# Pooling mixer: the product ahead of the trailing means, ScalarE copies gates and keys, half a u block between gates

## The chip, the cores and the metric

One core of one Trainium2 chip runs the whole program. The metric is the device time of one execution in microseconds (us); the number given for a kernel is the median of several runs. TensorE (PE) does matmuls and transposes, VectorE (DVE), ScalarE (ACT) and GpSimd (POOL) the elementwise work, SyncE (SP) starts most transfers. Each engine has its own instruction stream, and they wait for each other through semaphores (`wait_ge`, `then_inc`).

## The reference, cut to what matters

The program is one inference step of a two-layer encoder trunk on 544 tokens of 1,024 features: 512 frames of a new stream (prompt) and 32 frames of a running one (sample). Layer 0 mixes by a gated MLP (A) next to a sliding-window attention (B), layer 1 by trailing means (C). A SwiGLU FFN follows each mixer. Around each part stand an RMSNorm before and one after.

```python
def spatial_gate(u, va, ws, bs):                       # mixer A
    z = einsum('hij,bnjhc->bnihc', masked(ws), va) + bs
    return u * z
def pool_mixer(xn, hist, pos, c_w, c_scale):           # mixer C; hist: 15 older frames (zeros for the prompt)
    ext = concatenate([hist, xn])
    cs = pad(cumsum(ext))
    for g, w in enumerate((2, 4, 8, 16)):              # four groups of 256 features
        win_sum = cs[HIST+1 : HIST+1+t, g] - cs[HIST+1-w : HIST+1-w+t, g]
        diffs[g] = win_sum / minimum(pos + 1, w) - xn[:, g]
    return einsum('btgc,gce->btge', diffs, c_w) * c_scale, ext[-15:]
h = h + rms_norm(pool_mixer(rms_norm(h, g0)), g1)
h = h + rms_norm((silu(x @ w_gate) * (x @ w_up)) @ w_out, g3)      # x = rms_norm(h, g2)
```

The mean over a window is linear in the frames and the product with `c_w` is linear in the features, so either may come first.

## The kernel before, in words

**Products.** All data is f32. A matrix is split into a high and a low part, and `product` (lines 574 to 576) issues three matmuls: high by high, high by low, low by high. Features lie on the 128 partitions, tokens along the columns. The tokens are cut into half a (256 frames) and half b (256 frames and the 32 of the sample, 288 columns).

**Weights.** Weights come in units of 8 blocks of 128 columns. SP loads a unit into `raw` (3 buffers); ACT's `hi_part(m)` (L1124) rounds it into `whi`, DVE's `lo_part(m)` (L1541) forms `wlo` as the difference (4 buffers each). When PE is through with unit m, ACT and DVE prepare unit m + 4.

**Passes and slots.** After the front (mixers A and B of layer 0) come the FFN passes: `gu` (gate and up products) and `fo` (product with `w_out`), each over one half, for layer 0 `gu` a, `gu` b, `fo` a, `fo` b, for layer 1 `gu` a, `gu` b, `fo` b, `fo` a. One unit of a pass is a slot. What else has to be done in a pass is hung between its slots by the table `STAGE`: for a norm s (1: before mixer C, 2: before the FFN of layer 1) and a half, it names the slot of each step, and `stepper` lets each engine run the steps that are due after its part of a slot (`LATER` is half a slot later, on ACT). Steps of one engine thus stand in its stream behind the unit's own work, and a step that waits holds up what stands behind it.

- `sum`, `spread`, `fold`, `pre`, `again`: sums of squares by matmuls with ones, and the `spread` of 1/rms over the partitions by matmuls with the identity (L841).
- `scale` and `x`: DVE scales two feature tiles (L1837); ACT rounds them to `xhi`, DVE's `x_low` (L1846) forms `xlo`.
- `rows`, `keep`, `bands`: the pooling of mixer C. `turn_rows` (L973) transposes h on PE to frames on the partitions, ACT's `keep_rows` (L1439) scales it by 1/rms into `rows_a`, `rows_b`; PE's `band` (L996 to L1001; L989 for the sample with its history) multiplies with constant band matrices, which gives mean minus frame, back with features on the partitions. ACT's `band_high` and DVE's `band_low` split it. Half a does this in the `fo` pass of half b of layer 0 (norm 1, half a), half b in the `gu` pass of half a of layer 1.
- `pool_products`: two units of `c_w` (`c` units), placed in the pass by `C_AFTER`; a tile of its output goes through a ring of PSUM banks (`POOL_RING`, four for half a and three for half b) and is evacuated by ACT's `evacuate_z`, which also writes the squares for the next norm.

**Front.** PE does the blocks of va, then five heads q0 to q3 and k (`r` = 0 to 4), with transposes of v, `ws`, the key cache and the new keys between them. DVE applies the rotation of each head in `rope_step(r)`. `gate(a)` is PE's product of va with `wm_t`; DVE's `bias_gate(a)` adds the bias. Gates 0 and 1 stand after head 3, gates 2 and 3 after head 4 (gate 3 waits until `bias_gate(0)` has freed bank 0); then comes the loop over attention chunks, in which PE does scores, transposes and values of a chunk, and between them steps of the u block (`u_step`, six matmuls each, as many as `U_STEPS` says), and DVE `shift`, ACT the exponentials. `fill(n, bank)` (L592) issues n matmuls of the identity whose result nobody reads.

Lines of before that the steps below touch:

```python
fill(FILL_ROPE, 7)                 # PE, r == 3
pe.wait_ge(wm_ready, 1)
pe.wait_ge(kc_ready, 1)
...
dve.tensor_copy(wm_t[0:CHUNK, :, :], turned[0:CHUNK])          # DVE, rope_step(2)
dve.tensor_copy(wm_t[CHUNK:P, :, CHUNK:P], turned[CHUNK:P, :, CHUNK:P]).then_inc(wm_ready, 1)
dve.tensor_copy(k_s[:, CHUNK:P], flat(5, 0, CHUNK)).then_inc(kc_ready, 1)
...
bias_gate(2)
bias_gate(3)
lo_part(13)                        # then the loop with shift(c)
```

Of the kernel before, what the change touches and what calls it, by code (L numbers as in the profile page):

```python
# [60 lines left out]
U_STEPS = (3, 3, 2, 3, 3, 2, 3, 3, 2, 4, 4)  # L61
# [3 lines left out]
GATE_BANKS = (0, 2, 4, 0)  # L65
# [15 lines left out]
FILL_ROPE, FILL_GATE, FILL_TAIL = 20, 5, 4  # L81
# [4 lines left out]
BAND_ENTRIES = (tuple(range(KC)), (0, 1, 2, 3, "sample", 4, 5, 6, 7))  # L86
CARRY = 16
# [69 lines left out]
KEPT = {(0, 0): 1, (0, 1): 2, (1, 0): 3, (2, 0): 4, (2, 1): 5, (3, 0): 6}  # L157
# [49 lines left out]
def shape_constants():  # L207
# [11 lines left out]
    return np.concatenate([np.eye(P, dtype=np.float32), cos, sin, pooling_matrices()], axis=1)  # L219


def pooling_matrices():


    j, i = np.arange(P)[:, None], np.arange(P + CARRY)[None, :]
    row_at = np.concatenate([np.arange(DEC), np.arange(-HIST, 0)])[:, None]
    first, later, sample = [], [], []
    for w in POOLS:
        inside = (j <= i) & (j > i - w)
        count = np.where(i < P, np.minimum(i + 1, w), w)  # L230
        first.append(inside / count - (i == j))
        later.append(inside / w - (i == j))
        rows = np.zeros((P, DEC))
        at = np.arange(DEC)[None, :]
        rows[:DEC + HIST] = ((row_at <= at) & (row_at > at - w)) / w - (row_at == at)
        sample.append(rows)
    return np.concatenate(first + later + sample, axis=1).astype(np.float32)


def build(nc, x_prompt, x_sample, cache_k, cache_v, state, norm_g, ab_w_in, ln_g, ln_b, a_ws, a_bs, b_sinks,  # L240
          ab_w_out, c_w, c_scale, ffn_w_in, ffn_w_out, constants,
          y_p, y_s, bk_p, bv_p, cp_p, bk_s, bv_s, cp_s, av_s):
    with ExitStack() as ctx:
# [327 lines left out]
        def _(pe):  # L571
# [374 lines left out]
            def ring_wait(b, n):  # L946
# [3 lines left out]
                if back < 0:  # L950
                    return
# [1164 lines left out]
```

## Time and profile before

| | |
|---|---|
| median of three runs | 1049.93 us (1049.64, 1049.93, 1051.5) |
| profiled execution | 1051.53 us, of which the span of instructions is 1049.2 us |
| PE busy | 1031.9 us (98% of the span) |
| DVE busy | 621.2 us (59%) |
| ACT busy | 514.4 us (49%) |
| POOL busy | 48.1 us (5%) |
| mean granted clock of PE | 0.998 of full speed |
| moved by DMA | 162.47 MB, mean 155 GB/s |

Times in rows of the trace count from the start of the span. A row in order of time gives the start, the length from the first instruction's begin to the last one's end, the engine, the line of the kernel, the operation, `out<-in` by the program's names, the shapes, the number of instructions, and in brackets the idle time before it with what ended it. Matmuls overlap in the array, so a matmul's own length (0.28 us for 256 columns) is longer than its turn in the stream. Fills and gates count two instructions for each of their matmuls.

### The profile page before, as it was taken

Reading aid. Unit: us, or ns where it says so; the run is one execution under the profiler, and the core shown is the slowest. Engines: PE = TensorE matmul, PEld = TensorE weight load, DVE = VectorE, ACT = ScalarE, POOL = GpSimd, SP = SyncE. Lnnn points to the kernel's source line nnn. Section 1 sums busy time; section 2 is a strip of 40 time slices with the busy share of each in tenths; the row PEclk is TensorE's granted clock in tenths of the full one; section 3 lists DMA queues with packets and bytes.
Section 4 is the critical chain, followed back from the end, with each engine's and each line's share of the span. In section 5 each row is a group of like instructions: output and inputs, shape, how many; then the busy total and the mean of one; then the engine's idle time right before and its main releaser. Section 6 shows DMA issues by size and latency. Waiting matters only on the chain.

```text
span 1049.2 us, 19401 instructions
## 1 busy us (share of the span) xinstructions
PE 1031.9 (98%) x8097; PEld 1013.4 (97%) x8097; DVE 621.2 (59%) x923; ACT 514.4 (49%) x846; POOL 48.1 (5%) x52
## 2 busy tenths in 40 slices
PE   7999999999999999999999999999999999999997
PEld 6898799899999999999999999999999999999997
DVE  5397854887555555545465777557854555444643
ACT  6622365655444444444457565565544444444552
POOL 0080210000000000000000000200000000000000
PEclk9999999999999999999999999999999999999999
DMA  8322122566666555546664586445665555455554
GB/s 273 82 75 76 42 61 82 159 183 181 184 190 171 165 166 169 164 133 184 181 185 121 163 229 191 127 141 168 184 173 164 168 169 153 136 167 167 158 163 151
DMA packets 307925, 162.47 MB, mean 155 GB/s; under 512 B 14586, under 2 KB 304354, under 8 KB 307839
## 3 DMA queue, kind: packets, MB, share of 16 engines
q1 hardware_dynamic: 307374, 160.78, 52.7%
q8 instruction: 64, 1.05, 0.4%
q0 software_dynamic: 224, 0.35, 0.1%
q14 instruction: 23, 0.18, 0.1%
q10 hardware_dynamic: 240, 0.10, 0.0%
HBM read 158.63 MB, written 2.58 MB: 154 GB/s over the span
## 4 chain that ended last, share of the span: by engine, by line
PE 91%; DVE 5%; ACT 1%; issue 1%; DMA 1%; POOL 0%; ACTq 0%; DVEq 0%
PE ps L574 29%; PE ps L576 28%; PE ps L575 28%; DVE wlo L1541 1%; PE ps L830 1%; PE ps L841 1%; DMA gain_rows<-in_c_scale_dram 1%; PE ps L1001 0%; PE ps L973 0%; PE ps L996 0%; DVE va L1606 0%; DVE s_sb L1715 0%; DVE top L1709 0%; DVE den L1725 0%; DVE tmp L1837 0%
## 5 line engine op out<-in xcount | busy, mean ns | idle before, releaser
L1541 DVE TENSOR_TENSOR wlo<-raw,whi 128x1024 fp32r<-128x1024 f32 (+2 forms) x332 | 369.6, 1114 | 272.1 <-ACT whi L1124 271.7
L574 PE MATMUL ps<-xhi,whi 128*128 128x288 f32 (+1 forms) x1600 | 465.7, 291 | 3.0 <-DVE xlo L1846 1.6
L575 PE MATMUL ps<-xlo,whi 128*128 128x288 f32 (+1 forms) x1600 | 461.5, 288 | 0.0
L576 PE MATMUL ps<-xhi,wlo 128*128 128x288 f32 (+1 forms) x1600 | 459.1, 287 | 0.0
L1124 ACT ACTIVATE whi<-raw 128x1024 fp32r<-128x1024 f32 (+2 forms) x332 | 316.2, 955 | 229.0 <-PE ps L576 214.6
L574 PEld LDWEIGHTS ps<-xhi,whi 128*128 128x128 f32 x1600 | 301.2, 188 | 6.0 <-DVE xlo L1846 2.0
L576 PEld LDWEIGHTS ps<-xhi,wlo 128*128 128x128 f32 x1600 | 302.1, 189 | 0.0
L575 PEld LDWEIGHTS ps<-xlo,whi 128*128 128x128 f32 x1600 | 301.5, 188 | 0.0
L574 PE MATMUL ps<-mhi_b,whi 128*128 128x288 f32 x352 | 104.9, 298 | 0.0
L576 PE MATMUL ps<-mhi_b,wlo 128*128 128x288 f32 x352 | 104.3, 296 | 0.0
L575 PE MATMUL ps<-mlo_b,whi 128*128 128x288 f32 x352 | 102.7, 292 | 0.0
L574 PE MATMUL ps<-mhi_a,whi 128*128 128x256 f32 x352 | 99.9, 284 | 0.0
L576 PE MATMUL ps<-mhi_a,wlo 128*128 128x256 f32 x352 | 99.5, 283 | 0.0
L575 PE MATMUL ps<-mlo_a,whi 128*128 128x256 f32 x352 | 99.2, 282 | 0.0
L1386 ACT ACTIVATE tmp<-ps 128x256 f32<-128x256 f32 (+1 forms) x88 | 34.9, 397 | 124.4 <-PE ps L576 120.1
L575 PEld LDWEIGHTS ps<-mlo_b,whi 128*128 128x128 f32 x352 | 67.0, 190 | 0.0
L574 PEld LDWEIGHTS ps<-mhi_a,whi 128*128 128x128 f32 x352 | 66.6, 189 | 0.0
L575 PEld LDWEIGHTS ps<-mlo_a,whi 128*128 128x128 f32 x352 | 66.4, 189 | 0.0
L574 PEld LDWEIGHTS ps<-mhi_b,whi 128*128 128x128 f32 x352 | 66.2, 188 | 0.0
L576 PEld LDWEIGHTS ps<-mhi_b,wlo 128*128 128x128 f32 x352 | 66.0, 187 | 0.0
L576 PEld LDWEIGHTS ps<-mhi_a,wlo 128*128 128x128 f32 x352 | 66.0, 187 | 0.0
L1914 DVE TENSOR_TENSOR tmp<-tmp,ps 128x256 f32<-128x256 f32 (+1 forms) x88 | 38.5, 437 | 37.4 <-PE ps L576 37.3
(219 smaller groups left out, 932.6 us busy)
## 6 DMA issues: line engine op xcount, KB each, us to landing
raw<-in_ffn_w_in_dram SPq DMA_DIRECT2D x176, 512.0 KB, 3.9
raw<-in_ffn_w_out_dram SPq DMA_DIRECT2D x64, 384.0 KB, 3.5
raw<-in_ffn_w_out_dram SPq DMA_DIRECT2D x64, 320.0 KB, 3.1
raw<-in_ab_w_in_dram SPq DMA_DIRECT2D x10, 512.0 KB, 4.4
raw<-in_ab_w_out_dram SPq DMA_DIRECT2D x10, 256.0 KB, 2.9
raw<-in_ab_w_out_dram SPq DMA_DIRECT2D x20, 128.0 KB, 3.1
x_tok<-in_x_prompt_dram SPq DMA_DIRECT2D x4, 512.0 KB, 7.3
raw<-in_ab_w_in_dram SPq DMA_DIRECT2D x8, 256.0 KB, 3.8
```

The lines of the kernel that those rows point to most:

```text
L574: pe.matmul(out, wh, xh, start=first, stop=False)
L575: pe.matmul(out, wh, xl, start=False, stop=False)
L576: return pe.matmul(out, wl, xh, start=False, stop=last)
L830: mm = pe.matmul(flat(6 + b, i, 1, n), acc[:, 0, t0:t0 + n], ones[:, :], start=True, stop=True)
L841: mm = pe.matmul(flat(6 + b, P + i * P, w), lhs, ident[:, P - w:P], start=True, stop=True)
L1124: act.activation(whi[:, m % NSPLIT, 0:n], raw[:, m % NRAW, 0:n], ACT.Copy).then_inc(w_hi, 1)
L1386: act.activation(tmp[:, f % 2, c], flat(bank, 0, n), ACT.Silu).then_inc(silu_done, 1)
L1541: dve.tensor_tensor(wlo[:, s, 0:n], raw[:, m % NRAW, 0:n], whi[:, s, 0:n].bitcast(F32), ALU.subtract)\
L1914: dve.tensor_tensor(tmp2[:, f % 2, c], tmp[:, f % 2, c], flat(bank, 0, n), ALU.mult)\
```

## The change

**Mixer C.** The product with `c_w` now comes first, on the normalised frames, and the trailing means are formed from its output with the features on the partitions. Norm 1 gets steps like those before an FFN (`again`, `x`: DVE scales by the gains and 1/rms, ACT and DVE split), and the `c` units follow. ACT copies each output tile into `wide_a` or `wide_b`, behind 15 columns of history (POOL: zeros for half a, the last 15 columns of half a for half b). DVE's `window_step` adds a shifted copy 1, 2, 4, 8 columns back: one step for the first group, four for the last. `mix` scales the sum and subtracts the product itself (for half a after a multiplication of the first 15 columns with tabled counts), ACT's `mixed_out` writes the scaled result and its squares, `add_z` the sums. All of `rows`, `keep`, `bands` and their PE transposes and band matmuls go, with their constants. For the sample, its 15 frames of history are loaded as rows, turned by `turn_hist` and appended to half b's operand, which gets 304 columns; `turn_rows` remains for the 64 last frames alone, which are an output, and POOL scales them. The `c` units stand earlier in their passes (`C_AFTER`), and the steps of norms 1 and 2 lie in other slots.

**Front.** ACT copies `wm_t` and `k_s` after its `hi_part(10)`; DVE no longer does. The two fills of 20 and 5 go. Four steps of the u block (half of one block of features) are put between gate 2 and gate 3, which writes bank 6 and waits for no bias; the loop has four u steps fewer in all.

```diff
-U_STEPS = (3, 3, 2, 3, 3, 2, 3, 3, 2, 4, 4)
+U_FIRST = 4
+U_STEPS = (2, 2, 2, 3, 2, 2, 2, 3, 2, 4, 4)
...
-GATE_BANKS = (0, 2, 4, 0)
+GATE_BANKS = (0, 2, 4, 6)
...
-C_AFTER = ((15, 16), (22, 24))
+X_GAIN = ((0, 2), (1, 0), (1, 2))
+LAST_ROWS = 2 * DEC
+Z_COLS = (HIST + P * 2, 2 * HIST + P * 2 + DEC)
+C_AFTER = ((11, 12), (18, 20))
 STAGE = {
-    (1, 0): {"sum": 0, "spread": 1, "scale": (1, 2, 3, 4), "fold": 6, "pre": 8, "rows": (7, 7, 8, 8),
-             "keep": (9, 9, 10, 10), "bands": (11, 11, 12, 12, 13, 13, 14, 14)},
-    (2, 0): {"sum": 20, "spread": 21, "scale": (21, 22, 23, 24), "fold": 26, "pre": 28, "again": 29,
-             "x": (29, 30, 31, 32)},
-    (1, 1): {"sum": 2, "spread": 4, "scale": (4, 5, 7, 8), "fold": 10, "pre": 12, "rows": (10, 11, 11, 15, 15, 16),
-             "keep": (14, 14, 15, 15, 16, 16), "bands": (17, 17, 18, 18, 19, 19, 20, 20, 21)},
-    (2, 1): {"sum": 28, "spread": 30, "scale": (30, 31, 33, 34), "fold": 36, "pre": 38, "again": 40,
-             "x": (40, 41, 42, 43)},
+    (1, 0): {"sum": 0, "spread": 1, "scale": (1, 2, 3, 4), "fold": 5, "pre": 7, "again": 8, "x": (8, 9, 10, 11),
+             "windows": (13, 15, 16), "ends": (14, 17), "post": (14, 15, 17, 18), "add": (15, 17, 18, 20)},
+    (2, 0): {"sum": 22, "spread": 23, "scale": (23, 24, 25, 26), "fold": 28, "pre": 29, "again": 30,
+             "x": (30, 31, 32, 33)},
+    (1, 1): {"sum": 2, "spread": 4, "scale": (4, 5, 7, 8), "fold": 10, "pre": 12, "again": 14, "x": (14, 15, 16, 17),
+             "hist": 9, "rows": (10, 11), "keep": (15, 16),
+             "windows": (20, 23, 24), "ends": (21, 25), "post": (21, 22, 25, 26), "add": (22, 24, 26, 27)},
+    (2, 1): {"sum": 29, "spread": 31, "scale": (31, 32, 34, 35), "fold": 37, "pre": 39, "again": 41,
+             "x": (41, 42, 43, 44)},
...
+                if UNITS[m] == ("gu", 1, 0, 4):
                     sp.wait_ge(w_used, FO_PASS[0, 1][-1] + 1)
...
+                    sp.dma_start(hist[0:HIST, :], state[0, 0]).then_inc(hist_loaded, 16)
+                    sp.dma_start(hist[HIST:HIST + 1, :], state[0, 0, HIST - 1:HIST, :]).then_inc(hist_loaded, 16)
+                    sp.dma_start(gain_row[:, :], norm_g[1, 0].partition_broadcast(LAST_ROWS)).then_inc(hist_loaded, 16)
...
-                if a < 3:
-                    pe.wait_ge(rope_cosined, a + 2)
-                else:
-                    pe.wait_ge(gate_biased, 1)
+                pe.wait_ge(rope_cosined, a + 2)
...
-                    fill(FILL_ROPE, 7)
-                    pe.wait_ge(wm_ready, 1)
+                    pe.wait_ge(wm_ready, 2)
...
-                    fill(FILL_GATE, bank)
...
-                        pe.wait_ge(gate_biased, 4)
+                        pe.wait_ge(gate_biased, 1)
...
+            for n in range(U_FIRST):
+                u_step(n)
+            gate(3)
...
+            def turn_hist():
+                pe.wait_ge(hist_loaded, 48)
+                for k in range(KC):
+                    mm = pe.transpose(flat(4, k * DEC, HIST + 1), hist[:, k * P:(k + 1) * P], ident[0:HIST + 1, 0:HIST + 1])
+                mm.then_inc(hist_turned, 1)
+            def turn_rows(i):
+                pe.wait_ge(h_added[1], 8)
+                if i:
+                    pe.wait_ge(hist_lo, 1)
                 for q in range(4):
+                    mm = pe.transpose(flat(5 - i, q * P, P, LAST_ROWS), h[:, 4 * i + q, TOK - LAST_ROWS:TOK], ident[:, :])
+                mm.then_inc(rows_turned, 1)
...
+                n = width(b) + (HIST + 1 if b else 0)
+                cols = slice(b * CUT, b * CUT + n)
                 pe.wait_ge(w_lo, m + 1)
+                if b and j == 0:
+                    pe.wait_ge(hist_lo, 1)
+                    pe.wait_ge(rows_kept, 2)
+                    pe.wait_ge(r_kept[0], KEPT[2, 1])
                 for e in range(4 * j, 4 * j + 4):
                     g, o = divmod(e, 2)
...
+                    ring = POOL_RING[b]
+                    if e >= len(ring):
+                        pe.wait_ge(wide_kept[b], e - len(ring) + 1)
+                    pe.wait_ge(x_lo_done[b], 4 + g + 1)
                     for k in range(2):
                         w = slice(((g % 2 * 2 + k) * 2 + o) * P, ((g % 2 * 2 + k) * 2 + o + 1) * P)
-                        mm = product(flat(ring_bank(b, n), 0, width(b)), whi[:, s, w], wlo[:, s, w],
-                                     xhi[:, 2 * g + k, frames(b)], xlo[:, 2 * g + k, frames(b)], k == 0, k == 1)
+                        mm = product(flat(ring[e % len(ring)], 0, n), whi[:, s, w], wlo[:, s, w],
+                                     xhi[:, 2 * g + k, cols], xlo[:, 2 * g + k, cols], k == 0, k == 1)
                     mm.then_inc(w_used if e % 4 == 3 else pool_done[b], 1)
...
+                if m == 10:
+                    act.wait_ge(ws_turned, 1)
+                    turned = flat(4, 0, 512).rearrange("p (h i) -> p h i", h=AH)
+                    act.wait_ge(set_gaps, 1)
+                    act.activation(wm_t[0:CHUNK, :, :], turned[0:CHUNK], ACT.Copy).then_inc(wm_ready, 1)
+                    act.activation(wm_t[CHUNK:P, :, CHUNK:P], turned[CHUNK:P, :, CHUNK:P], ACT.Copy).then_inc(wm_ready, 1)
+                    act.wait_ge(kc_turned, 1)
+                    act.activation(k_s[:, CHUNK:P], flat(5, 0, CHUNK), ACT.Copy).then_inc(kc_ready, 1)
...
+                act.wait_ge(lead_set[b], 1)
                 for e in range(4 * j, 4 * j + 4):
                     if e % 4 == 3:
                         act.wait_ge(w_used, m + 1)
                     else:
                         act.wait_ge(pool_done[b], e - e // 4 + 1)
-                    bank = pool_bank(b, 2 * len(POOL_ROWS[b]) + len(BAND_ENTRIES[b]) + e)
-                    evacuate_z(2, b, e, (z_a, z_b)[b][:, e, :], flat(bank, 0, width(b)), c_gain[:, e:e + 1], scale_c(e))
+                    bank = POOL_RING[b][e % len(POOL_RING[b])]
+                    wide = (wide_a, wide_b)[b][0][:, e, :]
+                    if b:
+                        act.activation(wide[:, HIST + 2 * P:2 * HIST + 2 * P], flat(bank, 2 * P + DEC, HIST), ACT.Copy)
+                        act.activation(wide[:, 2 * HIST + 2 * P:], flat(bank, 2 * P, DEC), ACT.Copy)
+                    act.activation(wide[:, HIST:HIST + 2 * P], flat(bank, 0, 2 * P), ACT.Copy).then_inc(wide_kept[b], 1)
...
+            def mixed_out(b, e):
+                act.wait_ge(mixed[b], e // 2 + 1)
+                wide, out = (wide_a, wide_b)[b][0], (z_a, z_b)[b]
+                squares = acc[:, 0, frames(b)] if e == 0 else tmp2[:, e % 2, frames(b)]
+                pieces = ((HIST, 0, 2 * P),) + (((2 * HIST + 2 * P, 2 * P, DEC),) if b else ())
+                if e == 0:
+                    act.wait_ge(rstd_done[b], 4)
+                if e >= 3:
+                    act.wait_ge(z_added[b], add_count(2, e - 2))
+                for at, to, n in pieces:
+                    act.activation(out[:, e, to:to + n], wide[:, e, at:at + n], ACT.Copy, scale=c_gain[:, e:e + 1])
+                for at, to, n in pieces:
+                    op = act.activation(squares[:, to:to + n], wide[:, e, at:at + n], ACT.Square, scale=scale_c(e))
+                op.then_inc(z_out[b], 1)
...
+            def window_step(b, n, step, first, last):
+                wide = (wide_a, wide_b)[b]
+                lo = (1, 3, 7, 15)[step]
+                back, end = 1 << step, Z_COLS[b]
+                if step:
+                    dve.wait_ge(summed_up[b], n)
+                at = lambda i, k: k - 2 if i == 2 else k
+                src, dst = (0, 1, 2, 1)[step], (1, 2, 1, 2)[step]
+                s = slice(at(src, first), at(src, last))
+                dve.tensor_tensor(wide[dst][:, at(dst, first):at(dst, last), lo:end], wide[src][:, s, lo:end],
+                                  wide[src][:, s, lo - back:end - back], ALU.add).then_inc(summed_up[b], 1)
+            def windows(b, part):
+                if part == 0:
+                    dve.wait_ge(wide_kept[b], 4)
+                    window_step(b, 0, 0, 0, 4)
+                    window_step(b, 1, 1, 2, 4)
+                elif part == 1:
+                    dve.wait_ge(wide_kept[b], 8)
+                    window_step(b, 2, 0, 4, 8)
+                    window_step(b, 3, 1, 4, 8)
+                else:
+                    window_step(b, 4, 2, 4, 8)
+                    window_step(b, 5, 3, 6, 8)
+            def mix(b, half):
+                wide = (wide_a, wide_b)[b]
+                groups = range(2 * half, 2 * half + 2)
+                ends = [wide[1 + g % 2][:, 2 * g - 2 * (g % 2):2 * g - 2 * (g % 2) + 2, :] for g in groups]
+                dve.wait_ge(summed_up[b], (2, 6)[half])
+                if b == 0:
+                    dve.wait_ge(carry_kept, half + 1)
+                    dve.wait_ge(counts_loaded, 16)
+                    for g, s in zip(groups, ends):
+                        lead = s[:, :, HIST:2 * HIST]
+                        dve.tensor_tensor(lead, lead, counts[:, g:g + 1, :].broadcast_to([P, 2, HIST]), ALU.mult)\
+                            .then_inc(counted, 1)
+                    dve.wait_ge(counted, 2 * half + 2)
+                for g, s in zip(groups, ends):
+                    y = wide[0][:, 2 * g:2 * g + 2, HIST:Z_COLS[b]]
+                    dve.scalar_tensor_tensor(y, s[:, :, HIST:Z_COLS[b]], 1.0 / POOLS[g], y, ALU.mult, ALU.subtract)\
+                        .then_inc(mixed[b], 1)
...
+                steps = [(slot, 0, part) for part, slot in enumerate(at["windows"])]
+                steps += [(slot, 1, half) for half, slot in enumerate(at["ends"])]
+                steps += [(slot, 2, p) for p, slot in enumerate(at["add"])]
+                for slot, kind, n in sorted(steps):
                     yield slot
-                    band_low(b, i)
+                    if kind == 0:
+                        windows(b, n)
+                    elif kind == 1:
+                        mix(b, n)
+                    else:
+                        add_z(2, b, 2 * n)
+                        add_z(2, b, 2 * n + 1)
...
+            pool.wait_ge(w_used, FO_PASS[0, 0][-1] + 1)
+            pool.memset(wide_a[0][:, :, 0:HIST], 0.0).then_inc(lead_set[0], 1)
+            for half in range(2):
+                k = slice(4 * half, 4 * half + 4)
+                pool.wait_ge(wide_kept[0], 4 * half + 4)
+                pool.tensor_copy(carry[:, k, :], wide_a[0][:, k, 2 * P:2 * P + HIST]).then_inc(carry_kept, 1)
+            pool.wait_ge(w_used, FO_PASS[0, 1][-1] + 1)
+            pool.wait_ge(carry_kept, 2)
+            pool.tensor_copy(wide_b[0][:, :, 0:HIST], carry[:, :, :]).then_inc(lead_set[1], 1)
```

## Rows read from the trace of the kernel before

**Rows 1.** The page, part 1: busy us (share of the span) and instructions of each engine.

```profile
PE 1031.9 (98%) x8097; PEld 1013.4 (97%) x8097; DVE 621.2 (59%) x923; ACT 514.4 (49%) x846; POOL 48.1 (5%) x52
```

**Rows 2.** PE in order of time, front: start us, us, what [idle before <-releaser].

```profile
68.70 4.63 PE L592 MATMUL ps<-ident 128*128 128x128 f32 x40
73.89 0.36 PE L574 MATMUL ps<-xhi,whi 128*128 128x256 f32 x1 [0.56 <-DVE k_s L1662]
...
88.82 2.81 PE L662 MATMUL ps<-wm_t,va 128*128 128x128 f32 x20
...
94.41 0.35 PE L574 MATMUL ps<-xhi,whi 128*128 128x256 f32 x1 [0.82 <-DVE gated L1673]
...
146.49 0.39 PE L574 MATMUL ps<-yhi,whi 128*128 128x256 f32 x1 [0.81 <-DVE ylo L1769]
```

**Rows 3.** DVE in order of time, before the attention loop.

```profile
89.03 0.77 DVE L1622 STREAM_SHUFFLE tmp<-ps 128x544 f32<-128x544 f32 x1
...
93.48 0.68 DVE L1670 TENSOR_TENSOR gated<-ps,acc 128x512 f32<-128x512 f32 x1
...
94.18 1.22 DVE L1541 TENSOR_TENSOR wlo<-raw,whi 128x1024 fp32r<-128x1024 f32 x1
95.31 0.48 DVE L1709 TENSOR_REDUCE top<-ps 128x2 f32<-128x128 f32 x2
```

**Rows 4.** ACT in order of time, 61 to 70 us.

```profile
61.36 2.96 ACT L1124 ACTIVATE whi<-raw 128x1024 fp32r<-128x1024 f32 x3
```

**Rows 5.** PE in order of time, pooling of half a.

```profile
546.45 1.94 PE L973 MATMUL ps<-ident,h 128*128 128x128 f32 x16
...
554.58 0.41 PE L996 MATMUL ps<-band_first,rows_a 128*128 128x144 f32 x2
...
556.10 0.30 PE L575 MATMUL ps<-mlo_b,whi 128*128 128x288 f32 x1
```

**Rows 6.** PE in order of time, statistics and pooling of half b.

```profile
626.09 0.75 PE L841 MATMUL ps<-ident,rs 128*128 128x128 f32 x6
...
626.88 0.28 PE L575 MATMUL ps<-xlo,whi 128*128 128x256 f32 x1
...
671.57 0.41 PE L996 MATMUL ps<-band_later,rows_b 128*128 128x144 f32 x2
...
673.52 0.28 PE L575 MATMUL ps<-xlo,whi 128*128 128x256 f32 x1
...
676.34 1.97 PE L989 MATMUL ps<-band_sample,rows_b 47*128 47x32 f32 x16
```

**Rows 7.** Three stretches: length us, busy us (instructions) of PE, PEld, DVE, ACT, POOL, granted clock.

```profile
196.00:198.00 2.00, 1.16 (x10) 1.14 (x10) 1.93 (x5) 1.58 (x2) 0.00 (x0) 1.00 0.63 181
679.40:682.80 3.40, 3.40 (x19) 3.40 (x18) 2.05 (x3) 1.73 (x3) 0.00 (x0) 0.51 0.02 6
700.00:720.00 20.00, 20.00 (x169) 19.95 (x168) 13.03 (x19) 11.94 (x22) 0.87 (x1) 1.00 0.65 184
```

**Rows 8.** PE: first matmul of layer 1's `gu` pass of half a.

```profile
611.21 0.28 PE L574 MATMUL ps<-xhi,whi 128*128 128x256 f32 x1
```

**Rows 9.** DVE in order of time, start of layer 1; one heavy `gu` slot.

```profile
612.55 0.46 DVE L1797 TENSOR_TENSOR acc<-acc,tmp 128x288 f32<-128x288 f32 x1
...
749.52 0.42 DVE L1914 TENSOR_TENSOR tmp<-tmp,ps 128x256 f32<-128x256 f32 x1 [0.29 <-PE ps L576]
749.85 0.94 DVE L1837 SCALAR_TENSOR_TENSOR tmp<-h,gains,r_pre 128x288 f32<-128x288 f32 x2
750.71 0.75 DVE L1846 TENSOR_TENSOR xlo<-tmp,xhi 128x576 fp32r<-128x576 f32 x1
751.38 1.22 DVE L1541 TENSOR_TENSOR wlo<-raw,whi 128x1024 fp32r<-128x1024 f32 x1
```

**Rows 10.** ACT in order of time, 547 to 549 us.

```profile
547.52 1.26 ACT L1439 ACTIVATE rows_a<-ps,rs 128x512 f32<-128x512 f32 x2
```

**Rows 11.** The page, part 6, DMA issues: KB each, median us to landing.

```profile
raw<-in_ffn_w_in_dram SPq DMA_DIRECT2D x176, 512.0 KB, 3.9
```

More of the change, by code:

```diff
@@ L218, in shape_constants, with first_counts @@
             sin[p] = np.sin(ang[:, d % (ROPE // 2)]) * (-1.0 if d < ROPE // 2 else 1.0)
[L219 to L237, printed above, removed]
+    return np.concatenate([np.eye(P, dtype=np.float32), cos, sin, first_counts()], axis=1)
+def first_counts():
+    i = np.arange(1, HIST + 1)
+    rows = [np.maximum(w / i, 1.0) for w in POOLS]
+    return np.tile(np.concatenate(rows).astype(np.float32), (P, 1))
 def build(nc, x_prompt, x_sample, cache_k, cache_v, state, norm_g, ab_w_in, ln_g, ln_b, a_ws, a_bs, b_sinks,
@@ L708, in _ @@
             gate(2)
-            gate(3)
             def scores(c):
@@ L824, in sum_squares @@
                         pe.wait_ge(rstd_done[b], 2 * s)
-                short = pre and s == 1
                 for i, t in enumerate(POOL_ROWS[b]):
-                    t0, n = TILES[t]
-                    if not short:
-                        t0, n = t0 + n - P, P
-                    mm = pe.matmul(flat(6 + b, i, 1, n), acc[:, 0, t0:t0 + n], ones[:, :], start=True, stop=True)
+                    end = sum(TILES[t])
+                    mm = pe.matmul(flat(6 + b, i, 1), acc[:, 0, end - P:end], ones[:, :], start=True, stop=True)
+                if (s, b, pre) == (1, 1, 1):
+                    mm = pe.matmul(flat(7, 3, 1, LAST_ROWS), acc[:, 0, TOK - LAST_ROWS:TOK], ones[:, :],
+                                   start=True, stop=True)
                 mm.then_inc(sq_summed[b], 1)
@@ L1038, in pooling @@
             def pooling(b):
-                yield from norms(1, b)
-                for i, slot in enumerate(STAGE[1, b]["rows"]):
-                    yield slot
-                    turn_rows(b, i)
-                for i, slot in enumerate(STAGE[1, b]["bands"]):
-                    yield slot
-                    band(b, i)
+                at = STAGE[1, b]
+                yield at["sum"]
+                sum_squares(1, b, 0)
+                yield at["spread"]
+                spread(1, b, 0)
+                if b:
+                    yield at["hist"]
+                    turn_hist()
+                    for i, slot in enumerate(at["rows"]):
+                        yield slot
+                        turn_rows(i)
+                yield at["pre"]
+                sum_squares(1, b, 1)
+                yield at["again"]
+                spread(1, b, 1)
                 yield from norms(2, b)
@@ L1275, in root @@
                 act.wait_ge(sq_summed[b], stat_count(s, pre))
[L1276 to L1279 removed]
+                n = len(POOL_ROWS[b])
                 act.activation(ms[:, 3 * b:3 * b + n], flat(6 + b, 0, n), ACT.Sqrt, bias=eps[:, :]).then_inc(rooted[b], 1)
@@ L1369, in ffn_in @@
                     act.wait_ge(out_stored, 16 * STORES_AB)
+                if b == 0 and layer == 1:
+                    act.wait_ge(carry_kept, 2)
                 if b == 1 and layer == 1:
@@ L1489, in norms @@
                     yield slot + LATER
-                    x_high(s // 2, b, p)
+                    x_high(s, b, p)
+                    if (s, b) == (1, 1) and p in (1, 2):
+                        yield at["keep"][p - 1] + LATER
+                        keep_rows(p - 1)
             def pooling(b):
                 yield from norms(1, b, b)
-                for i, slot in enumerate(STAGE[1, b]["keep"]):
-                    yield slot
-                    keep_rows(b, i)
-                for i, slot in enumerate(STAGE[1, b]["bands"]):
-                    yield slot
-                    band_high(b, i)
+                for p, slot in enumerate(STAGE[1, b]["post"]):
+                    yield slot + LATER
+                    mixed_out(b, 2 * p)
+                    mixed_out(b, 2 * p + 1)
                 yield from norms(2, b, b)
```

260 lines of the change are left out of this document (73 added, 187 removed).

## The prediction

> **What bounds the kernel now.** I read the page first, then the engines in order of time around each place that the diff touches, then windows for the granted clock. TensorE (PE) is busy 98% of the span and VectorE (DVE) 59%, ScalarE (ACT) 49% [rows 1]; so whatever leaves PE's stream is time won, as long as PE finds its operands ready. Two kinds of places have to be kept apart. In the FFN passes PE runs back to back, 169 matmuls of mostly 256 columns in 20 us [rows 7], one every 0.118 us, and so one of 288 every 0.13; there a removed matmul counts in full. In the front, PE twice does work that nobody needs (`fill`) and then still waits for DVE [rows 2]; behind that lies the attention loop, where DVE and ACT hand each chunk to and fro and PE only follows. There PE's saving counts only as far as DVE starts its loop earlier.
>
> **Front.** PE issues 20 fills at 68.70 and goes on with the next head at 73.89, after a wait for DVE's copy into `k_s` [rows 2]. The copies of `wm_t` and `k_s` go to ACT behind its third `hi_part`, which is over at 64.3 [rows 4]; three copies of 512 columns or less at some 0.6 us each [rows 10] end by 66, before PE needs them. So this head, gates 0 and 1 and the next head move up by 73.89 − 68.73 = 5.16 us, and the last head ends at 88.82 − 5.16 = 83.66. Two gates take 2.8 us there [rows 2]. After the change follow gate 2 (1.4, to 85.05), half a u block (24 matmuls × 0.118 = 2.8, to 87.9) and gate 3 (to 89.3). DVE's chain restarts 0.2 us after the last head [rows 2, 3] and reaches the bias of gate 2 at 88.3; the bias of gate 3 must now wait for PE, 89.5, takes 0.7, `lo_part` 1.13, and the first `shift` starts at 91.35 in place of 95.31 [rows 3]. The gain is **4.0**, not the 5.16 + 2.2 = 7.3 that PE no longer spends (2.2 is what 88.82 to 94.41 holds beyond gates 2.75 and scores 0.67 [rows 2]). Inside the loop PE has four u steps less, but DVE does not start an iteration sooner for that; the freed PE time is idle. Bounds: 0 if the loop ends at its old time, 7.3 if it starts with PE.
>
> **Half a.** Four turns of rows are 16 transposes: a stretch of 1.94 us, less the 0.13 that an ordinary matmul there takes anyway and an estimated 0.07 for the change of kind, 1.74 [rows 5]. Eight bands come in four stretches like 554.58 to 556.10, less 0.13: 1.39 each, 5.55 together [rows 5]. New is one `spread` of two columns: that of three costs 626.09 to 626.88 less 0.12 = 0.67 [rows 6], so 0.45. Net −1.74 − 5.55 + 0.45 = **−6.8**.
>
> **Half b.** Two bands cost 673.52 − 671.57 − 0.12 = 1.83, eight 7.3; the sample band 1.95 [rows 6]; 24 transposes at 1.74/16, 2.6. Right behind the sample band, whose sixteen instructions move few columns, the granted clock is 0.51 for 3.4 us, the level of 1.2 GHz, though PE is busy throughout [rows 7]; that loses 3.4 × 0.49 = 1.65 and goes with its cause. New: `spread` 0.67; eight small history transposes, at most 0.108 each as the large ones, 0.85; eight transposes of the 64 last frames, 0.85; one more statistics column, 0.15; 48 product matmuls 16 columns longer, 16/2.4 GHz × 48 = 0.3. Net −(7.3 + 1.95 + 2.6 + 1.65) + 2.8 = **−10.7**; if the small transposes called for the lower clock themselves, −9.
>
> **What takes it back.** The windows go to DVE. Its durations come from one heavy `gu` slot: up product 0.33, scaling 0.86, low part of a pair 0.67 [rows 9]; `lo_part` is 1.13 for 1024 columns (94.18 to 95.31, [rows 3]), so about 1.05 ns a column and 0.06. A `window_step` over four channel tiles is 1,268 columns in half b, 1.4; over two, 0.73; a `mix` of two groups 1.4. `lo_part` of a unit runs some three slots before PE reads it, which hides a backlog of several us, but three places are short:
> - Second product unit of half b (slot 22). ACT's `mixed_out` for tiles 0 and 1 stands at slot 21, ahead of the evacuation of that unit, and needs DVE's first `mix`. Counted from PE's end of slot 20: DVE up product 0.5, windows 0 2.25, `lo_part` 1.15, low part 0.35, first STT 0.75, so 5.1; ACT then needs eight small activations, 1.7 (256 columns at half of rows 10's 0.58, the 32 at 0.1), and evacuates tile 4 by 7.4. PE ends slot 21 at 2.85, and has only three banks: tile 7 can start at 2.85 + 3 × 0.83 = 5.3 and waits for tile 4's bank until 7.4. **+2.1**, between 0.5 and 3.5. In half a the same `mixed_out` stands behind the unit and there are four banks: no wait.
> - Start of layer 1's `gu` pass. All steps of norm (2, 0) move a slot; the last `x_low` leaves the `fo` pass. The pass starts at 611.21 [rows 8]. From 612.55 DVE adds 0.37 [rows 9], scales 0.8, low part 0.6, `lo_part` 1.13, last low part 0.7: pair 2 is ready at 614.35, pair 3 at 616.2, where PE wants them at 614.05 and 615.5 (1.42 a pair). **+0.7**.
> - Slots 13 to 21 of half a. My count by the same durations has DVE deliver unit 21's low part 0.2 us before PE wants it. **+0.3**, between 0 and 1.5.
>
> The other parts I cost at nothing. SP's three history loads now wait for the end of the `fo` pass four units earlier and hold up the load of `gu` 4: issued by 612.5, landed 3.9 later [rows 11], with both parts (1.0 and 1.13) ready at 618.6, wanted at 611.2 + 4 × 2.85 = 622.6. POOL's product of the last rows stands ahead of its `power` of slot 39, but begins after slot 36, with 8.5 us to spare. The count load at the start and POOL's copies of 15 columns are small beside the transfers and steps around them; should one be late, the mix of half a is, by as much.
>
> **Sum.** −4.0 − 6.8 − 10.7 + 2.1 + 0.7 + 0.3 = −18.4. The profiled execution took 1051.53 (span 1049.2 and 2.3 around it); that gives 1033.1 on its scale. The median of the runs shown is 1.6 below it, so **1031.5**.
>
> **Rivals.**
> - *PE stays fed.* DVE's `mix` is in time, or ACT faster than I count: the 3.1 us of waits vanish and the time is 1028.5; if the front gave its bound too, 1025.2. For it: DVE idles 41% of the span [rows 1]. Against: my count leaves nothing out that would be faster. Chance 0.2.
> - *More waits or a lower clock.* The waits come out larger (up to 3 us more), or the clock falls once in the thinner attention loop and once behind the 2 us wait, 1.65 each [rows 7]: 1034.8. For it: a stretch of little work cost 3.4 us of low clock. Against: at 196 to 198 PE was busy 1.16 of 2 us and kept 1.00 [rows 7]. Chance 0.26.
> - *The move to ACT does nothing.* If ACT's copies came behind its next `hi_part`, PE would wait as before: front 0, 1035.5. Against: the code puts them ahead of that wait. Chance 0.02.
> - *Slower.* The clock drops at the first gap of the attention loop and stays low in it, since DVE's pace keeps making gaps. Each us at the low level loses half of itself; 37 us of it eat the 18.4. The stretch 94.41 to 146.49 [rows 2] is long enough: low over all of it costs 26, some 1057.5. Against: no stretch of this trace stays low. Chance 0.02.
>
> In the Trainium skill, "TensorE: Matmul & The Clock Gate", section "A second HAM failure mode: psum-queue depth-cycling" says that short idle gaps between groups of matmuls can make the clock swing between half and full rate. By that rule the loop, which has more gaps after the change, would see several drops; with two the sum would end at 1034.8, the second rival. The row at 196 us speaks against it, so I keep its chance low.
>
> **Numbers.** The likeliest case holds 0.5. From it at 1031.5, the fed PE at 1028.5 down to 1025.2, and the more troubled one up to 1036, I take 1026.5 to 1036.5. 0.2% (2.1 us) is about what a measurement of this kernel can tell from no change; all cases but the last are faster by more: 0.97 faster, 0.01 same, 0.02 slower.
>
> **What would show it.** Right: PE goes from the k transposes straight into the next head; `shift` starts near 91.3; PE idles in the loop by 0.5 to 1 us an iteration; no low clock behind half b's pooling; one PE wait of about 2 us for ACT in the second product unit of half b, a few tenths for `xlo` at the start of layer 1's `gu` pass. Wrong: a first `shift` near 95, PE waiting for `wlo` in half a's windows, or low clock in the loop.

## The result, and the profile after

| | before | after |
|---|---|---|
| median | 1050.01 us (4 runs, 1049.64 to 1051.5) | 1040.11 us (4 runs, 1038.1 to 1043.01) |
| profiled execution | 1051.53 us, span 1049.2 | 1043.01 us, span 1041.2 |

The ratio is 0.990, with a 95% interval of 0.9887 to 0.9914: 9.9 us faster. The forecast was 1031.5 with a range of 1026.5 to 1036.5; the sign was right, the size was not.

The page of the changed kernel, part 1 (busy us, share of the span, instructions):

```profile
PE 1017.6 (98%) x7907; PEld 997.9 (96%) x7907; DVE 640.1 (61%) x952; ACT 518.9 (50%) x875; POOL 51.9 (5%) x55
```

Beside [rows 1]: PE is busy 14.3 us less, but the span shrank by 8.0 only: 6.3 us of idle time came in. Busy time also holds what PE does at the low clock, of which this execution has more than that of before (next part), so 14.3 understates the work that left its stream. The shares do not show the idle time, as PE is 98% busy before and after; the list of PE's waits does. Two executions of the changed kernel agree in it but for some tenths. Lines of before, and of the run `after_again` below, which is the changed kernel once more (what waits <- for whom: sum in us, times, longest):

```profile
PE ps L574 <- DVE xlo L1846: 1.6, 2, 0.8
PE ps L756 <- POOL s_sb L2057: 1.6, 3, 0.8
...
PE ps L830 <- DVE acc L1815: 0.8, 1, 0.8
```

```profile
PE ps L729 <- POOL s_sb L2046: 3.2, 4, 1.4
PE ps L554 <- ACT pooled_b L1407: 2.6, 1, 2.6
PE ps L554 <- DVE xlo L1793: 2.0, 3, 0.8
PE ps L803 <- DVE acc L1762: 1.8, 2, 1.1
PE ps L554 <- DVE u_raw L1696: 1.3, 2, 1.1
...
PE ps L803 <- DVE acc L1744: 0.5, 1, 0.5
PE ps L817 <- DVE rs L1726: 0.3, 1, 0.3
```

In the changed kernel L803 is the sum of squares, L817 `spread`, L729 the transposes of the attention loop, L554 the first of three product matmuls. Of the lines shown, before has those for `s_sb`, `acc` and `xlo`, and none of the others.

**Falls of the clock.** The execution profiled first has three stretches at the low level while PE works. Windows of it (length, busy us and instructions of PE, PEld, DVE, ACT, POOL, granted clock, DMA share, GB/s):

```profile
100.00:102.00 2.00, 2.00 (x11) 2.00 (x11) 1.17 (x4) 0.72 (x2) 0.00 (x0) 0.50 0.03 8
598.00:600.00 2.00, 2.00 (x10) 2.00 (x10) 0.83 (x1) 0.10 (x1) 0.00 (x0) 0.50 0.75 205
684.00:686.00 2.00, 2.00 (x11) 2.00 (x11) 1.23 (x1) 2.00 (x6) 0.00 (x0) 0.51 0.00 0
```

Each stretch loses 1.7 us (the sum of what windows of 1 us show missing from 1.00), like the one of [rows 7], and each stands close behind a wait of PE, in order of time:

```profile
95.61 0.60 PE L729 MATMUL ps<-ident,s_sb 128*64 128x128 f32 x4 [0.58 <-POOL s_sb L2046]
98.81 0.49 PE L554 MATMUL ps<-xhi,whi 128*128 128x256 f32 x1 [1.07 <-DVE u_raw L1696]
...
596.56 0.61 PE L803 MATMUL ps<-ones,acc 128*128 128x1 f32 x4 [1.47 <-DVE acc L1762]
...
681.82 0.41 PE L554 MATMUL ps<-xhi,whi 128*128 128x304 f32 x1 [2.56 <-ACT pooled_b L1407]
```

They are no fixed part of the kernel: `after_again` has the same waits and not one fall, and 1037.54 us. Nor is the fall of before: of 21 executions of before beside the first experiments, 12 took 1049.7 to 1050.2 us and 9 took 1051.1 to 1051.7. Two variants of before with its time (below) were profiled in either kind: `moved_x`, 1051.16 us, has the low stretch at 678 to 682 us, `off64`, 1049.94 us, has none. The forecast was made against an execution of the second kind, and the median is of the first.

**Where the time went.** Without falls the two kernels can be laid side by side. `off64` is before with 64 unused bytes on each partition and the same time (below); its profile has no fall. Windows between the same first matmuls of the passes, first `off64`, then `after_again`: front, layer 0's `gu` a, layer 0's `fo` b, layer 1's `gu` a, all behind it.

```profile
41.61:191.87 150.26, 145.69 (x1156) 136.77 (x1154) 106.89 (x223) 62.91 (x120) 34.16 (x28) 1.00 0.27 74
191.87:321.18 129.31, 127.67 (x1080) 127.25 (x1081) 89.21 (x124) 67.91 (x103) 2.66 (x2) 1.00 0.65 186
525.34:611.19 85.85, 85.85 (x670) 85.85 (x669) 59.40 (x95) 53.00 (x105) 0.00 (x0) 1.00 0.55 162
611.19:759.02 147.83, 147.83 (x1252) 147.43 (x1251) 104.32 (x149) 85.85 (x140) 10.55 (x9) 1.00 0.61 173
759.02:1047.60 288.58, 283.06 (x2194) 282.53 (x2192) 140.78 (x180) 126.21 (x197) 0.00 (x0) 1.00 0.55 161
```

```profile
41.56:187.57 146.01, 139.89 (x1105) 131.02 (x1104) 105.64 (x220) 63.89 (x123) 34.20 (x28) 1.00 0.28 76
187.57:317.98 130.41, 128.77 (x1080) 128.36 (x1081) 89.28 (x124) 67.91 (x103) 2.66 (x2) 1.00 0.64 185
522.13:603.86 81.73, 79.87 (x611) 79.18 (x609) 67.52 (x110) 51.84 (x97) 1.22 (x3) 1.00 0.55 162
603.86:747.09 143.23, 140.26 (x1172) 139.41 (x1171) 115.37 (x165) 90.44 (x174) 12.23 (x9) 1.00 0.62 175
747.09:1035.70 288.61, 283.05 (x2194) 282.52 (x2192) 141.71 (x181) 126.12 (x197) 0.00 (x0) 1.00 0.54 161
```

| stretch | measured | forecast |
|---|---|---|
| front | −4.25 | −4.0 |
| layer 0 `gu` a | +1.10 | 0 |
| layer 0 `fo` b | −4.12 | −6.8 + 0.3 = −6.5 |
| layer 1 `gu` a | −4.60 | −10.7 + 1.65 (the fall that the median of before lacks) + 2.1 + 0.7 = −6.25 |
| sum | −11.9 | −16.75 |

The stretches left out (layer 0 `gu` b and `fo` a) take 204.16 and 204.15. The medians differ by 9.9 and not 11.9, as by their times most executions of the changed kernel have a fall or more, and most of before have none.

### The profile page after: what moved, and what is told of

The parts are those of the page before. It is cut to its first block, busy times and chain, and to the rows that moved or that the text cites. A ratio compares the mean times of both kernels' runs of the same rounds, so it can differ in the third digit from the quotient of the medians.

```text
span 1041.2 us, 19085 instructions
## 1 busy us (share of the span) xinstructions
PE 1017.6 (98%) x7907; PEld 997.9 (96%) x7907; DVE 640.1 (61%) x952; ACT 518.9 (50%) x875; POOL 51.9 (5%) x55
## 4 chain that ended last, share of the span: by engine, by line
PE 88%; DVE 7%; ACT 2%; issue 1%; DMA 1%; SPq 0%; POOL 0%; DVEq 0%; ACTq 0%
PE ps L554 28%; PE ps L556 28%; PE ps L555 28%; DVE wlo L1500 2%; DVE tmp L1784 1%; PE ps L803 1%; DMA x_tok<-in_x_prompt_dram 1%; ACT whi L1069 1%; PE ps L817 1%; DVE xlo L1793 1%; PE ps L638 0%; DVE s_sb L1666 0%; DVE den L1676 0%; DVE top L1660 0%; PE ps L593 0%
## 5 line engine op out<-in xcount | busy, mean ns | idle before, releaser
L554 PE MATMUL ps<-xhi,whi 128*128 128x256 f32 (+1 forms) x1600 | 468.1, 293 | 6.0 <-ACT pooled_b L1407 2.6
L556 PE MATMUL ps<-xhi,wlo 128*128 128x256 f32 (+1 forms) x1600 | 462.0, 289 | 0.0
L555 PE MATMUL ps<-xlo,whi 128*128 128x256 f32 (+1 forms) x1600 | 461.1, 288 | 0.0
L554 PEld LDWEIGHTS ps<-xhi,whi 128*128 128x128 f32 x1600 | 302.1, 189 | 9.6 <-DVE xlo L1793 2.9
L554 PE MATMUL ps<-mhi_b,whi 128*128 128x288 f32 x352 | 105.3, 299 | 0.0
L554 PE MATMUL ps<-mhi_a,whi 128*128 128x256 f32 x352 | 100.0, 284 | 0.0
L554 PEld LDWEIGHTS ps<-mhi_b,whi 128*128 128x128 f32 x352 | 66.9, 190 | 0.0
L554 PEld LDWEIGHTS ps<-mhi_a,whi 128*128 128x128 f32 x352 | 66.6, 189 | 0.0
```

The lines of the kernel that those rows point to most:

```text
L554: pe.matmul(out, wh, xh, start=first, stop=False)
L555: pe.matmul(out, wh, xl, start=False, stop=False)
L556: return pe.matmul(out, wl, xh, start=False, stop=last)
```

## The experiments

**Parts alone.** `front_alone` is before with the diff's edits of the front, `pool_alone` the changed kernel with the front of before:

```diff
-                    fill(FILL_ROPE, 7)
-                    pe.wait_ge(wm_ready, 1)
+                    pe.wait_ge(wm_ready, 2)
...
+            for n in range(U_FIRST):
+                u_step(n)
+            gate(3)
```

> The kernel before with the front's edits alone (ACT copies, no fills, half a u block ahead of gate 3). Theory: DVE's first shift comes 4 us earlier than before, as in the changed kernel, but the clock falls once in the attention loop and PE waits there, so that the products of the mixers' output begin only about 2.5 us earlier: 1047.5 us. Rival 1, the loop keeps all of the head start: 1046.0. Rival 2, the loop gives all of it back: 1050.0.

1045.78 us, ratio 0.9961 (0.9948 to 0.9973): 4.4 faster, rival 1. Its profile has one fall, at 97 to 102 us, and is the slowest of the five executions (1047.17); by the others the front is worth the whole head start of DVE, whose first `shift` comes at 90.97 us for 95.31.

> The changed kernel with the front of before (DVE copies, both fills, old gates and u steps). Theory: all of the missing gain but 1.5 us is lost behind the front, so the time is 1042.6 us (1040.1 + 2.5), with the same three PE waits: two at the statistics of the norm behind mixer C of half a (0.5 and 1.5 us), one in the second product unit of half b (2.6 us). Rival, the parts disturb each other (the earlier start shifts the transfers): the waits are gone and the time is below 1040.

1041.75 us, ratio 0.9921 (0.9907 to 0.9934): 8.4 faster, with the three waits at 0.5, 1.1 and 2.6 us. The waits do not come from the earlier start; the rival falls. That 4.4 and 8.4 make more than 9.9 is not cleared up by the falls alone: by the times the median of the whole holds one or more and that of `front_alone` none, but the profile of `pool_alone`, its median execution, has one too (680 to 684 us). This execution also begins the front 1.1 us earlier than `off64` (40.53 us for 41.61), which `after_again` does not (41.56). Stretch by stretch the parts add better: with its fall of 1.7 taken out, `pool_alone` wins 8.4 us in the three passes of the table and the changed kernel 7.6, and the front of `pool_alone` takes as long as that of `off64` (150.27 and 150.26).

**The changed kernel once more.**

> The changed kernel once more, unchanged, for the spread of its times. Theory: its runs differ by whole falls of the clock of 1.7 us each, so they lie near 1038.1 (none), 1039.8 (one), 1041.5 (two) and 1043.2 (three), with the median at 1040, and the trace shows as many low stretches as the time says, each behind one of PE's waits. Rival: the times spread evenly, and the low stretches stand elsewhere.

1037.54, 1039.06, 1039.62, 1042.1 and 1042.76 us; ratio 0.9904 (0.9887 to 0.992). The steps are there only roughly, since the first transfers shift an execution by some tenths as well. The low stretches agree where a profile shows them: three at 1043.01 us, none at 1037.54. The executions between have no profile; one or two falls in them are read from the times alone.

**Rows of xhi.** Nothing in the forecast speaks of layer 0's `gu` pass, which the diff does not touch but for the rows of its operand: they grew from 544 to 560 columns to hold the history. `wide_x` gives the kernel before the longer rows (`xlo` as well):

```diff
-        xhi = sb("xhi", [P, KC, TOK], F32R)
+        xhi = sb("xhi", [P, KC, TOK + HIST + 1], F32R)
...
-        z = sb("z", [P, KC, TOK])
+        z = sb("z", [P, KC, TOK + HIST + 1])
```

> The kernel before with rows of xhi, xlo and z of 560 columns, as in the changed kernel, in place of 544, and nothing else changed (the 16 columns of carry lie in z). Theory: the longer rows alone slow the matmuls of 256 columns that read them, so layer 0's gu pass of half a takes 130.4 us in place of 129.3, layer 1's as much more, and the whole 1052.3 us. Rival, the rate comes from what the other engines do: 129.3 us and 1050.0.

1051.85 us, ratio 1.0017 (1.0009 to 1.0026). `wide_x`, `gu` a and `gu` b of layer 0:

```profile
191.47:321.87 130.40, 128.74 (x1080) 128.33 (x1081) 89.22 (x124) 67.91 (x103) 2.66 (x2) 1.00 0.64 184
321.87:462.66 140.79, 140.79 (x1059) 140.79 (x1058) 70.84 (x88) 59.79 (x88) 0.00 (x0) 1.00 0.55 160
```

The longer rows alone bring the +1.1 us, without any other work beside them. In layer 1's `gu` pass of half a they cost 0.8: 148.61 us (611.85 to 760.46) against the 147.83 of `off64`, neither with a fall.

> The kernel before with rows of 544 columns, but an unused tile behind xhi and carry behind z, so that all tiles behind them lie where they lie with the longer rows. Theory: not the place of the weights, but the distance of the rows counts, so the pass takes 129.3 us and the whole 1050.0. Rival, the places count: 130.4 us and 1052.3.

1050.02 us, ratio 0.9999 (0.999 to 1.0008), pass 129.34 us. The edit puts `sb("gap_hi", [P, KC, HIST + 1])` behind `xhi` and `carry` behind `z`. So it is not where the tiles behind lie.

> The kernel before with a tile of 16 columns ahead of xhi, so that every row of xhi and xlo begins 64 bytes further; the distance of the rows stays at 544 columns. In the wide_x kernel only every second row was so displaced, and the gu pass of half a took 1.06 us more. Theory: the place of a row's begin counts, so the pass takes 129.34 + 2 x 1.06 = 131.4 us and the whole 1053.5 to 1054. Rival, the distance between rows counts: 129.3 us and 1050.0.

1049.8 us, ratio 0.9997 (0.9988 to 1.0006), pass 129.31 us. The edit is `sb("gap", [P, 16])` ahead of `xhi`. My theory fell: the begin of a row does not count, the distance does.

> The kernel before with rows of xhi, xlo and z of 552 columns: 8 more than before, 8 fewer than in the changed kernel. With 544 the gu pass of half a takes 129.34 us, with 560 it takes 130.40. Theory: any distance other than 544 that is no whole multiple of 128 bytes slows the matmuls of 256 columns, so the pass takes 130.0 us or more and the whole 1051 to 1052. Rival, 560 alone is slow, or the loss grows only past some distance: 129.3 us and 1050.0.

1047.5 us, ratio 0.9971 (0.996 to 0.9982): faster than before, which neither theory had. `x_552`, the same two passes:

```profile
191.86:321.21 129.35, 127.69 (x1080) 127.29 (x1081) 89.34 (x124) 67.79 (x103) 2.66 (x2) 1.00 0.64 186
321.21:460.88 139.67, 139.67 (x1058) 139.67 (x1057) 70.88 (x88) 59.80 (x88) 0.00 (x0) 1.00 0.56 161
```

With 544 the passes of 256 columns are quick (129.3) and those of 288 slow (140.8), with 560 the first are slow as well (130.4), with 552 both are quick (129.35 and 139.7). Layer 1's `gu` b becomes quicker by as much as layer 0's (139.67 for 140.80). What rule lies behind it stays open; distances above 560 were not tried.

**The clock in the attention loop.** `fed_loop` is the changed kernel with

```diff
+                    if n == KC:
+                        fill(5, 7)
                     u_step(n)
...
+                if i == 1:
+                    pe.wait_ge(gate_biased, 4)
+                    fill(3, 7)
                 if 1 <= i <= NCH + 1:
                     turn_probs(i - 1)
```

> The changed kernel with 3 and 5 fills in PE's two waits at the start of the attention loop (ahead of the first turn of probabilities and of the second u block). Theory: the fall of the clock at 98 us comes from the gaps; with fills it is gone in every run, PE's time to the mixers' output shrinks by 1.7 against runs that had the fall, and the median is 1.0 to 1.7 us under the changed kernel's. Rival: the fills push out what PE is waited for, or the clock falls anyway: no gain, up to 1 us slower.

1037.1 us, ratio 0.9875 (0.986 to 0.9891): 2.5 under `after_again`, all four executions between 1036.4 and 1038.3. Windows of `after_again` and, below, `fed_loop`:

```profile
96.00:98.00 2.00, 0.93 (x11) 0.82 (x10) 1.71 (x6) 0.66 (x2) 0.61 (x1) 1.00 0.00 0
```

```profile
96.00:98.00 2.00, 2.00 (x21) 1.93 (x20) 1.71 (x6) 0.67 (x2) 0.61 (x1) 1.00 0.00 0
```

DVE's 1.71 us are the same, so the fills hold nothing up; against an execution without a fall they win nothing (1037.1 and 1037.54). Of the six profiles with this loop and no fills (`after`, `after_again`, `front_alone` and three of the next kernels) five have a fall there, `after_again` alone has none; of two with fills (`fed_loop`, `all_fed`) none has one.

**The waits.** The next kernels move entries of the table `STAGE`. `c1_steps`, half b of mixer C:

```diff
-             "windows": (20, 23, 24), "ends": (21, 25), "post": (21, 22, 25, 26), "add": (22, 24, 26, 27)},
+             "windows": (20, 23, 24), "ends": (21, 25), "post": (22, 23, 25, 26), "add": (23, 24, 26, 27)},
```

> The changed kernel with mixed_out of half b's first four tiles behind the second product unit alone (22, 23 in place of 21, 22; add_z 23 in place of 22). Theory: PE's wait of 2.6 us there and the fall of the clock that follows in some runs go; layer 1's gu pass of half a takes 1.7 to 2.6 us less than the 143.2 that it takes in the changed kernel without a fall, and the runs lie near 1035.5 to 1037.5 where the clock falls at most once. Rival: DVE or ACT is short of time there, so that the next unit's low part or the sums come late by as much: pass 143 us.

1036.38 us, ratio 0.9862 (0.9847 to 0.9877): 3.2 under `after_again`. The wait is gone and layer 1's `gu` a takes 141.19 us for 143.23:

```profile
606.70:747.89 141.19, 140.22 (x1173) 139.42 (x1171) 115.60 (x166) 90.48 (x174) 11.38 (x9) 1.00 0.62 178
```

Its profile has one long low stretch, 97 to 108 us, in the attention loop.

`fo_steps`, half a of mixer C and the norm behind it:

```diff
-             "windows": (13, 15, 16), "ends": (14, 17), "post": (14, 15, 17, 18), "add": (15, 17, 18, 20)},
-    (2, 0): {"sum": 22, "spread": 23, "scale": (23, 24, 25, 26), "fold": 28, "pre": 29, "again": 30,
+             "windows": (13, 15, 16), "ends": (14, 17), "post": (14, 15, 17, 18), "add": (15, 17, 18, 19)},
+    (2, 0): {"sum": 22, "spread": 23, "scale": (23, 24, 25, 26), "fold": 27, "pre": 29, "again": 30,
```

> The changed kernel with the last add_z at slot 19 and the fold at 27 alone, in layer 0's fo pass of half b. Theory: the wait of 0.5 us at the sum goes, the one at the fold shrinks from 1.1 to 0.7, and the pass, 81.7 us without a fall, shrinks by about 0.6; the runs lie under the changed kernel's by that and, where the clock fell in this pass, by 1.7 more: a median near 1038.5. Rival: the steps only change places with the low parts, and PE waits as long for those: 1039.6.

1039.38 us, ratio 0.9896 (0.9879 to 0.9913): no difference that can be told from `after_again`. The waits at the sum and at the fold are gone, but PE waited 0.98 us for DVE's 1/rms at the `spread` and 1.02 for the first `wlo` of the next pass; the pass took 81.47 us for 81.73. The rival was right.

```profile
581.57 0.71 PE L817 MATMUL ps<-ident,rs 128*128 128x128 f32 x4 [0.98 <-DVE rs L1726]
...
605.61 0.36 PE L554 MATMUL ps<-xhi,whi 128*128 128x256 f32 x1 [1.02 <-DVE wlo L1500]
```

`both_steps` has both edits:

> The changed kernel with steps moved in the table: the last add_z of half a's mixer C a slot earlier (19), the fold of the next norm a slot earlier (27), and mixed_out of the first four tiles of half b behind the second product unit (22, 23 in place of 21, 22; add_z 23). Theory: the missing gain behind the front is these three waits (0.5, 1.5 and 2.6 us) and the falls of the clock behind them; all go, so 1034 to 1035 us, with the fall in the attention loop left. Rival: DVE is short of time there, and the waits only move to the next step: 1038.5 or more.

1035.59 us, ratio 0.9862 (0.9842 to 0.9882), from 1033.56 to 1038.7; the slowest is the profiled one, with a low stretch of 97 to 108 us. The front took 2.9 us longer in it than in `after_again` (191.10 − 42.22 against 187.57 − 41.56). In `fo` b waits of 0.74 us at the fold and 0.89 for the first `wlo` are left.

`all_fed` has both and the fills of `fed_loop`:

> The changed kernel with all of these: the moved steps of both places and the eight fills in the attention loop. Theory: the effects add, so the median is 1033 us, with hardly any spread by falls of the clock, and PE's waits in the trace behind the front sum to 3 us. Rival: the fall of the clock moves to another place: median 1035 or more.

1034.51 us, ratio 0.9848 (0.9834 to 0.9861), 15.5 under before: the best version. Its four executions lie within 0.8 us and its profile has no fall. It is 1.5 above the forecast of the effects' sum; the pass of `fo` b takes 79.99 us, that of layer 1's `gu` a 141.56:

```profile
522.70:602.69 79.99, 79.71 (x610) 79.06 (x609) 66.69 (x108) 51.77 (x96) 1.42 (x4) 1.00 0.56 165
602.69:744.25 141.56, 140.29 (x1170) 139.49 (x1171) 115.89 (x167) 90.50 (x174) 11.20 (x9) 1.00 0.62 177
```

## Why the prediction was wrong

The median came out 8.6 us above the forecast of 1031.5. By the stretches, this is about 1.65 for a fall of the clock that was taken off twice, 2.0 for falls in the median of the changed kernel (11.9 − 9.9), 1.9 for longer rows, 1.6 for waits in `fo` b and 1.5 for work sized too high; the rest is small and partly cancels.

- **The wait list was short by one place.** "`lo_part` of a unit runs some three slots before PE reads it, which hides a backlog", with three exceptions: I asked of DVE's work only when the low parts come, and never when PE's own statistics want `acc`. There PE waited 0.5, 1.1 and 0.3 us without a fall, 1.9 in this pass where 0.3 was forecast, 1.6 of the 2.4 that `fo` b missed; the other 0.8 is work sized too high (below). And "All steps of norm (2, 0) move a slot" was not so: `sum` to `fold` move two slots, `pre` and what follows one, so `fold` to `pre` shrank from two slots to one. DVE and ACT of the changed kernel before the wait of 1.47 us:

```profile
592.97 0.95 DVE L1500 TENSOR_TENSOR wlo<-raw,whi 128x768 fp32r<-128x768 f32 x1
594.49 0.96 DVE L1500 TENSOR_TENSOR wlo<-raw,whi 128x768 fp32r<-128x768 f32 x1 [0.56 <-ACT whi L1069]
595.37 0.68 DVE L1756 TENSOR_TENSOR acc<-acc,tmp 128x512 f32<-128x512 f32 x1
596.08 0.42 DVE L1762 TENSOR_TENSOR acc<-acc 128x256 f32<-128x256 f32 x1
```

```profile
593.09 0.63 ACT L1259 ACTIVATE tmp<-h 128x512 f32<-128x512 f32 x1 [1.18 <-DVE h L1774]
593.63 1.52 ACT L1069 ACTIVATE whi<-raw 128x768 fp32r<-128x768 f32 x2
```

  The squares (L1259) are ready at 593.7, but DVE takes up the fold at 595.37, as a `lo_part` that waits for ACT's second `hi_part` stands ahead. Moving the step did not cure it (`fo_steps`): as much waiting came out elsewhere. The same edits leave 2.0 us of waits in `fo_steps`, 1.6 in `both_steps` and 0.3 in `all_fed`; why they help there and not alone is open.
- **Longer rows were costed at nothing.** They took 1.1 us in layer 0's `gu` a and, in `wide_x`, 0.8 in layer 1's. If the changed kernel pays the same there, that is half of what that pass missed (1.65).
- **The fall of the clock was counted as part of before.** The 1.65 us that "goes with its cause" is inside the −10.7, and the step from 1033.1 to the median took off another 1.6, so the same fall was counted twice. For the changed kernel I put "the clock falls once in the thinner attention loop and once behind the 2 us wait" into a rival at 0.26 and priced a fall at 1.65, where 1.7 is measured. The profiles show none and three, and one longer stretch in two variants. In the Trainium skill, "TensorE: Matmul & The Clock Gate", section "A second HAM failure mode: psum-queue depth-cycling" tells of a kernel in which short gaps between groups of matmuls make the clock swing; I held the row at 196 us against it. The runs agree with the page in the attention loop (five of six profiles, none of two with the gaps filled), while behind the waits in the passes the clock falls in some executions only: behind the 2.56 us in three of five profiles, behind the wait at the fold in one of five, the one where it took 1.47 us and not 1.1. A wait is not the only thing that goes ahead of a fall: in [rows 7] PE was busy throughout.
- **The second product unit** came as forecast, a little larger: +2.1 forecast, 2.56 measured, of which `c1_steps` gave back 2.04. The changed kernel's ACT in order of time, from `mixed_out` to the copies that free the banks (L1407):

```profile
678.80 0.72 ACT L1420 ACTIVATE z_b<-pooled_b,c_gain 128x256 f32<-128x256 f32 x2 [0.68 <-DVE pooled_b L1935]
679.43 0.70 ACT L1422 ACTIVATE acc<-pooled_b,gains 128x256 f32<-128x256 f32 x2
680.04 0.70 ACT L1420 ACTIVATE z_b<-pooled_b,c_gain 128x256 f32<-128x256 f32 x2
680.66 0.70 ACT L1422 ACTIVATE tmp<-pooled_b,gains 128x256 f32<-128x256 f32 x2
...
681.40 0.36 ACT L1407 ACTIVATE pooled_b<-ps 128x256 f32<-128x256 f32 x1
```

  ACT waits for DVE's `mix`, spends 2.5 us on the eight activations (forecast 1.7), and PE goes on at 681.82, when the first copy is over.

- **The front** was right: the first `shift` came at 91.06 us in `after_again` (91.35 forecast), and 4.25 us were won (4.0 forecast).

- **The work taken from PE** in mixer C was sized a little high. `all_fed` takes 5.86 and 6.27 us less than `off64` in the two passes (85.85 − 79.99, 147.83 − 141.56). The first still holds a wait of 0.28, the second waits of 1.05 and 0.16 and the 0.8 of the longer rows, so the work itself is 6.1 and 8.3, where 6.8 and 9.05 (10.7 − 1.65) were forecast. Which of the single costs was too high was not measured.
- **The small waits.** At the start of layer 1's `gu` pass the changed kernel waits 0.34 us and its variants up to 1.07 (forecast 0.7); the 0.3 for low parts among half a's windows did not come.

## What to carry to other kernels

Where a change makes an engine busier, list every step at which the bounding engine asks it for something, statistics and buffers as well as operands, and look at the distance between the step that makes a value and the step that wants it after all steps have moved. Look at whether the profiled execution is of the kind that the median stands for before a term is taken from a single stretch of it. A tile that only gets wider is a change of its own: compare a pass that the change leaves alone.

## What the runs showed that was not expected

- **Distance of rows.** The same matmuls, back to back, took 129.3 or 130.4 us a pass at 256 columns and 139.7 or 140.8 us at 288, by the distance of the operand's rows (544, 552, 560 columns), while shifting all rows by 64 bytes or the tiles behind them did nothing. 552 made the kernel before 0.29% faster (0.18 to 0.4%); the edit widens `xhi`, `xlo` and `z` and nothing else.
- **Falls of the clock in some executions only.** One and the same kernel was profiled with none and with three stretches at the low level, each losing 1.7 us; two variants of it have one of 97 to 108 us, and the front of one of these took 2.9 us longer. Eight useless matmuls of identity in PE's waits took those in the attention loop out of both profiles with them. The spread of the executions went from 5.2 us (`after_again`) to 1.9 (`fed_loop`).
